# Hybrid decoder block: input rows transposed unscaled, row scales applied at evacuation, the next block's convolution placed ahead of the scan

## The chip, the cores and the metric

The kernel runs on one core of a Trainium2 chip. The metric is the device time of one execution in microseconds (us), median of the runs.

## The reference

All in float32, 1024 tokens of width 1024:

```
h = RMSNorm(x);  [u_rnn | g_rnn | u_pool | q_mem] = h @ W_in        (1024 x 1536)
A (512 ch): u = causal depthwise conv(4)(u_rnn) + b
            r, i = sigmoid(u @ W_a + b_a), sigmoid(u @ W_i + b_i)   (per head, 64x64)
            a = exp(-8 r softplus(-lam)); h_t = a h_(t-1) + sqrt(1 - a^2) i u;  y = h * gelu(g_rnn)
B (256 ch): trailing means over 2/4/8/16 tokens minus the token, a map per group, a scale
C (256 ch): 4 heads of q_mem attend to keys and values of RMSNorm(mem) (256 rows)
x = x + concat(A, B, C) @ W_out;   x = x + MoE(RMSNorm(x))  (top 4 of 32 experts);  out = RMSNorm(x)
```

## The kernel before, in words

The program has two phases: the mixer (everything up to the router and the token lists, about the first 350 us) and the expert phase, which starts when the mixer is done. The change touches the mixer alone. Each engine has its own program, written out by hand, and runs it in order; semaphores join them, so the order of the text is the order of the work.

**Three products for one.** The large products are made as hi*hi + hi*lo + lo*hi: a float32 operand is split in a rounded part (a copy on ScalarE, "hi") and a rest (a subtraction on VectorE, "lo"). One projection `n` of the input matrix has 128 output channels: two halves of 512 tokens, 8 k-steps of three products each, so 24 products a half (L1057 to L1059).

**The head.** Ten row tiles of 128 rows (8 of `x`, 2 of `mem`) are loaded by SP into 7 slots. ScalarE squares and sums each tile (`square`, L429), VectorE makes the mean (L711), ScalarE the root (L434), VectorE the reciprocal (L707), ScalarE scales the identity matrix by it (`row_scale`, L448), and TensorE multiplies the tile with that scaled identity (`transpose_rows`, L1039), which transposes and normalizes at once. ScalarE makes the hi part of a tile's first bank (`x_hi`, L439), VectorE the hi part of the second and both lo parts (`xT_evac`, L722, L725). A table of 50 columns of weights (`vrows`, eight small loads that POOL issues at L357) is transposed at L1072 before tile 2 and copied to `vec` (L702); POOL scales the first two pieces of W_in by a column of it (L381, `scale`), ScalarE and VectorE split them (`w_in_hi` L457, `w_in_lo` L734). The first half of projection 0 comes after the transposes of tile 7.

**Keys and values.** SP loads the key/value weights (2 MB, L288) into the place of tiles 3 to 6 once they are transposed, then eight pieces of a bias (L291, L292), then W_in piece by piece (L274), each when its slot of three is free. VectorE scales pieces 2 and up (L738). `keys_values` (L1082, L1086) follows projection 1, and ScalarE copies its result out (L599, L601).

**The recurrence.** Four blocks `c` of 128 channels. TensorE: projection 2c (u), projection 2c+1 (g), then `gates(c)` (L1099, from the convolved u), with no pause between them; they need w_in_lo of the piece, and the banks of two projections before emptied. ScalarE: `root_of(c-1)` (L515), `u_evac(c)` (L486), w_in_hi(2c+2), `g_evac(c)` with the gelu (L496), w_in_hi(2c+3), `gate_values(c)` (sigmoid L504 and L506, tanh L509, exp L510), each change of function with a table load. VectorE, for each c: w_in_lo(2c+3); i*u (L826); L829 to L832; scale(2c+5); L835, L836, the scan (L837), the product with the gelu (L841, semaphore `rnn_done`); `conv(c+1)` (L807, L810); w_in_lo(2c+4); scale(2c+6).

**After it.** Projections 8 and 9 (pool), 10 and 11 (queries) are interleaved with the pooling windows (`pool_windows`, VectorE), the first scores and the split of W_out. Then eight token tiles go through the output product, second norm and router, and TensorE is fed without a gap until the mixer's end.

Of the kernel before, what the change touches and what calls it, by code (L numbers as in the profile page):

```python
# [67 lines left out]
def mixer_phase(nc, dram, scratch, shared):  # L68

    ctx = ExitStack()  # L70
    with ctx:
# [32 lines left out]
        def c_tile(i):  # L104
# [42 lines left out]
        scales = nc.alloc_sbuf_tensor_at("scales", [P, 2, P], F32, offset=start["b_gu_lo"])  # L147
# [3 lines left out]
        w_out_row = [rows[:, 0, :], rows[:, 1, :], rows[:, 2, :], w_out_h[:, :],  # L151
# [21 lines left out]
        gexp = sb("gexp", [P, TOPK])  # L173
        cnt = sb("cnt", [P, 8, E])
# [4 lines left out]
        ss2, ms2, sd2, rs2 = (small[:, 40 + i * 2:42 + i * 2] for i in range(4))  # L179


        rows_in = [sem(f"rows_in{i}") for i in range(7)]
# [6 lines left out]
        vecT_ready, vec_done, lam_abs, lam_exp, lam_done = (sem(n) for n in ("vecT_ready", "vec_done", "lam_abs", "lam_exp", "lam_done"))  # L189
        ss_done, ms_done, sd_done, xn_done, xT_ready, xT_done = (sem(n) for n in ("ss_done", "ms_done", "sd_done", "xn_done", "xT_ready", "xT_done"))  # L190
# [6 lines left out]
        out_ready, x2_done, ss2_done, ms2_done, sd2_done, h2_done, h2T_ready, h2T_done = (  # L197
            sem(n) for n in ("out_ready", "x2_done", "ss2_done", "ms2_done", "sd2_done", "h2_done", "h2T_ready", "h2T_done"))
# [10 lines left out]
        rs_done = sem("rs_done")  # L209
# [4 lines left out]
        row_slots = [rows[:, i, :] for i in range(3)] + [region_d[:, i * D:(i + 1) * D] for i in range(4)]  # L214

        def row_slot(item):

            n = len(row_slots)
            if item < NORMED:
                return item % n, item // n + 1  # L220
            return (item - NORMED) % 3, sum(i % n == (item - NORMED) % 3 for i in range(NORMED)) + (item - NORMED) // 3 + 1

        def row_tile(item):
            return row_slots[row_slot(item)[0]]
# [37 lines left out]
        def _(sp):  # L262
            def load_rows(item):

                if item < TT or item >= NORMED:
                    t = item if item < TT else item - NORMED
                    src = dram["x"][0, t * P:(t + 1) * P, :]
                else:
                    src = dram["mem"][0, (item - TT) * P:(item - TT + 1) * P, :]
                sp.dma_start(row_tile(item), src).then_inc(rows_in[row_slot(item)[0]], 16)  # L270
# [23 lines left out]
            for n in range(3, NPROJ):  # L294
# [9 lines left out]
                if n == 8:  # L304
                    sp.wait_ge(bias_set, 16 * 8)
                    for k in range(RT):
# [7 lines left out]
            load_w_out(6)  # L314
            sp.wait_ge(d_done, 2)
            load_w_out(7)
            sp.wait_ge(w_out_lo_done, KT + 3)
# [21 lines left out]
        def _(pool):  # L339
# [6 lines left out]
            vector_rows = [  # L346
                (V_CONVW, CONV * RT, dram["conv_w"][0].rearrange("w (c p) -> (w c) p", p=P)),
                (V_CONVB, RT, dram["conv_b"][0].rearrange("(c p) -> c p", p=P)),
                (V_BA, RT, dram["b_rg_a"][0].rearrange("(c p) -> c p", p=P)),
                (V_BI, RT, dram["b_rg_i"][0].rearrange("(c p) -> c p", p=P)),  # L350
                (V_LAM, RT, dram["lru_lambda"][0].rearrange("(c p) -> c p", p=P)),
                (V_PS, PT_, dram["pool_scale"][0].rearrange("(c p) -> c p", p=P)),
                (V_GMIX, KT, dram["norm_mix_g"][0].rearrange("(c p) -> c p", p=P)),
                (V_GMEM, KT, dram["mem_norm_g"][0].rearrange("(c p) -> c p", p=P)),
            ]
            for r, n, src in vector_rows:
                pool.dma_start(vrows[r:r + n, :], src).then_inc(vrows_in, 16)  # L357
# [66 lines left out]
        def _(act):  # L424
            def square(s):
                act.wait_ge(rows_in[row_slot(s)[0]], 16 * row_slot(s)[1])
# [5 lines left out]
            def root(s):  # L432
                act.wait_ge(ms_done, s + 1)
                nc.scalar.activation(sd[:, s:s + 1], ms[:, s:s + 1], ACT.Sqrt).then_inc(sd_done, 1)  # L434

            def x_hi(s):

                act.wait_ge(xT_ready, s + 1)
                nc.scalar.activation(hi_part[:, 0:4, s * P:(s + 1) * P],  # L439
                                     bank(4 + 2 * (s % 2))[:, 0, :].rearrange("p (k t) -> p k t", k=4),  # L440
                                     ACT.Copy).then_inc(x_hi_done, 1)

            def row_scale(s):

                if s >= 2:
                    act.wait_ge(xT_ready, s - 1)
                act.wait_ge(rs_done, s + 1)
                nc.scalar.activation(scales[:, s % 2, :], ident[:, :], ACT.Copy, scale=rs[:, s:s + 1]).then_inc(xn_done, 1)  # L448
# [9 lines left out]

            act.preload_act_table(ACT.Sqrt)
            square(0)  # L460
            square(1)
            act.wait_ge(consts, 1)
            root(0)
            for s in range(NORMED):
                if s + 2 < NORMED:
                    square(s + 2)
# [1570 lines left out]
```

## Time and profile before

| what | value |
|---|---|
| median of 3 runs | 1742.6 us (1738.94 to 1742.95) |
| the profiled execution, its own time | 1743.29 us |
| its span in the profile | 1741.6 us |
| TensorE busy | 1667.9 us, 96% of the span |
| VectorE / ScalarE / POOL busy | 75% / 63% / 27% |
| mean granted TensorE clock | 0.98 |

The profile gives one execution, in us from the start of the span. A row of the timeline has start, duration, engine, line, operation, output and inputs, count, and in brackets the idle time before it and what ended it. A busy TensorE is not one at its peak, since the durations of pipelined products overlap: the pace is read from start to start.

### The profile page before, as it was taken

The page shows a single profiled execution, that of the slowest core. Times are in us where ns is not written, and L with a number is a line of the kernel's source. Part 1 is how long each engine was busy: PE and PEld are TensorE (multiplying, and loading weights), DVE is VectorE, ACT ScalarE, POOL GpSimd, SP SyncE. Part 2 cuts the span into 40 slices and gives each one's busy share as a digit, 9 for nine tenths or more (in the row PEclk, how much of TensorE's full clock was granted, in tenths as well). Part 3 has the DMA queues.
Part 4 walks back from the last instruction along what each step waited for, and adds up shares of the span by engine and source line. Part 5 has one row for each costly group of instructions (what it writes and reads, how often), then busy time and mean ns, then how long its engine had stood idle before and what let it go on. Part 6 is the DMA issues. An engine that isn't in the chain of part 4 may idle for free.

```text
span 1741.6 us, 29439 instructions
## 1 busy us (share of the span) xinstructions
PE 1667.9 (96%) x8641; PEld 1242.4 (71%) x8642; DVE 1303.3 (75%) x1168; ACT 1103.9 (63%) x1074; POOL 463.9 (27%) x348
## 2 busy tenths in 40 slices
PE   6999999759999999999999999999999999999996
PEld 6877777546786768888868887678666767765674
DVE  5578656666787868998869997669668669665787
ACT  5455555355676758877758876567556657654674
POOL 5000002432322525322225222215213026123240
PEclk9999999869999999999999999999999999999998
DMA  9121132467898989999989998689868788887685
GB/s 281 52 97 58 52 110 73 170 237 288 329 346 326 350 316 350 389 380 385 391 321 351 390 375 324 232 347 378 307 263 296 299 326 324 296 319 259 227 324 218
DMA packets 114171, 485.64 MB, mean 279 GB/s; under 512 B 16430, under 2 KB 29040, under 8 KB 81360
## 3 DMA queue, kind: packets, MB, share of 16 engines
q1 hardware_dynamic: 96128, 445.58, 66.0%
q0 software_dynamic: 18000, 39.49, 9.3%
q8 instruction: 27, 0.44, 0.1%
q14 instruction: 16, 0.13, 0.0%
HBM read 451.79 MB, written 33.23 MB: 278 GB/s over the span
## 4 chain that ended last, share of the span: by engine, by line
PE 71%; DVE 3%; issue 2%; DMA 2%; ACT 1%; POOLq 0%; ACTq 0%; DVEq 0%; POOL 0%; SPq 0%
PE ps L1837 20%; PE ps L1839 18%; PE ps L1838 18%; PE ps L1852 6%; PE ps L1890 3%; DVE w_lo L1681 2%; PE ps L1810 2%; PE ps L1860 1%; DMA raw_weights<-in_w_down 1%; ACT w_hi L1535 1%; PE ps L1915 1%; DVE raw_weights L1782 0%; PE ps L1819 0%; DMA stand_in<-token_lists 0%; DVE raw_weights L1799 0%
## 5 line engine op out<-in xcount | busy, mean ns | idle before, releaser
L1681 DVE TENSOR_TENSOR w_lo<-raw_weights,w_hi 128x2048 fp32r<-128x2048 f32 x256 | 576.5, 2284 | 137.8 <-ACT w_hi L1535 137.8
L1535 ACT ACTIVATE w_hi<-raw_weights 128x2048 fp32r<-128x2048 f32 x256 | 485.5, 1911 | 219.7 <-DMA raw_weights<-in_w_gu 114.9
L1837 PE MATMUL ps<-w_hi,xT 128*128 128x512 f32 x1024 | 415.4, 406 | 10.7 <-issue 5.1
L1838 PE MATMUL ps<-w_lo,xT 128*128 128x512 f32 x1024 | 402.9, 393 | 0.0
L1839 PE MATMUL ps<-w_hi,xT 128*128 128x512 f32 x1024 | 402.4, 393 | 0.0
L1681 DVE TENSOR_TENSOR w_lo<-raw_more,w_hi 128x2048 fp32r<-128x2048 f32 x128 | 290.1, 2284 | 28.8 <-ACT w_hi L1535 28.2
L1837 PEld LDWEIGHTS ps<-w_hi,xT 128*128 128x128 f32 x1024 | 194.1, 190 | 91.4 <-issue 46.6
L1535 ACT ACTIVATE w_hi<-raw_more 128x2048 fp32r<-128x2048 f32 x128 | 244.2, 1908 | 0.3 <-DMA raw_more<-in_w_down 0.3
L1461 POOL DMA_INDIRECT x_rows<-h_rows,next_list x33 | 79.0, 2395 | 598.0 <-issue 598.0
L1839 PEld LDWEIGHTS ps<-w_hi,xT 128*128 128x128 f32 x1024 | 193.8, 189 | 42.7
L1838 PEld LDWEIGHTS ps<-w_lo,xT 128*128 128x128 f32 x1024 | 194.3, 190 | 36.7
L1837 PE MATMUL ps<-w_hi,hT 128*128 128x512 f32 x512 | 211.1, 412 | 1.0 <-DVE hT L1722 1.0
L1839 PE MATMUL ps<-w_hi,hT 128*128 128x512 f32 x512 | 201.0, 393 | 0.0
L1838 PE MATMUL ps<-w_lo,hT 128*128 128x512 f32 x512 | 199.8, 390 | 0.0
L1506 POOL DMA_INDIRECT acc_rows<-y,this_list x31 | 169.5, 5469 | 57.8 <-ACT y L1604 51.4
L1593 ACT ACTIVATE glu<-ps 128x512 f32<-128x512 f32 x64 | 38.2, 597 | 145.0 <-PE ps L1839 143.2
L1839 PEld LDWEIGHTS ps<-w_hi,hT 128*128 128x128 f32 x512 | 96.1, 188 | 22.1
L1837 PEld LDWEIGHTS ps<-w_hi,hT 128*128 128x128 f32 x512 | 96.1, 188 | 19.3 <-issue 1.5
L1838 PEld LDWEIGHTS ps<-w_lo,hT 128*128 128x128 f32 x512 | 96.5, 188 | 17.2
L418 POOL DMA_INDIRECT token_lists<-entry,sloti x32 | 32.7, 1023 | 284.5 <-DVE sloti L944 276.9
L1722 DVE TENSOR_TENSOR hT<-ps,hT 128x512 fp32r<-128x512 f32 x64 | 44.2, 691 | 61.3 <-ACT hT L1597 61.2
L1852 PE MATMUL ps<-raw_weights,xT_tail 128*32 128x512 f32 x720 | 82.6, 596 | 0.0
(318 smaller groups left out, 2134.9 us busy)
## 6 DMA issues: line engine op xcount, KB each, us to landing
raw_weights<-in_w_gu SPq DMA_DIRECT2D x192, 1024.0 KB
raw_more<-in_w_gu SPq DMA_DIRECT2D x64, 1024.0 KB, 6.7
raw_weights<-in_w_down SPq DMA_DIRECT2D x64, 1024.0 KB
raw_more<-in_w_down SPq DMA_DIRECT2D x64, 1024.0 KB, 11.6
rows<-in_x SPq DMA_DIRECT2D x12, 512.0 KB
w_in_sb<-in_w_in SPq DMA_DIRECT2D x12, 512.0 KB, 4.6
acc_rows<-region_c SPq DMA_DIRECT2D x8, 512.0 KB
h_rows<-region_c SPq DMA_DIRECT2D x8, 512.0 KB
```

Of the source, the lines that this page charges most:

```text
L1461: pool.indirect_dma_start(out=x_rows[:, :], out_offset=None, in_=scratch["h2"], in_offset=bass.IndirectOffsetOnAxis(ap=next_list[:, 0:1], ...
L1506: pool.indirect_dma_start(out=scratch["acc"], out_offset=bass.IndirectOffsetOnAxis(ap=this_list[:, 0:1], axis=0), in_=y[:, :], in_offset=N ...
L1535: S.activation(w_hi[:, j % RING, :], raw(j % RING), ACT.Copy).then_inc(hi_done, 1)
L1593: S.activation(glu[:, :], ps[:, 2 * half, :], ACT.Gelu_apprx_sigmoid).then_inc(glu_done, 1)
L1681: V.tensor_tensor(w_lo[:, j % RING, :], raw(j % RING), w_hi[:, j % RING, :].bitcast(F32), ALU.subtract).then_inc(lo_done, 1)
L1722: V.tensor_tensor(part[:, :, 1, :], rows_transposed(2 * half), part[:, :, 0, :].bitcast(F32), ALU.subtract)\
L1810: last = T.transpose(ps[:, 1 + 2 * half, k * P:(k + 1) * P], x_rows[:, (4 * half + k) * P:(4 * half + k + 1) * P], ident[:, :])
L1837: T.matmul(out, hi, hi_w, start=first, stop=False)
L1838: T.matmul(out, hi, lo_w, start=False, stop=False)
L1839: return T.matmul(out, lo, hi_w, start=False, stop=end)
L1852: last = T.matmul(ps[q * TAIL:(q + 1) * TAIL, BANK_TAIL + g, :].rearrange("p (a n) -> p a n", a=2), xT_tail[:, k, g * TAIL:(g + 1) * TAIL] ...
L1890: last = T.matmul(ps[(2 * h + e) * TAIL:(2 * h + e + 1) * TAIL, BANK_TAIL + g, :], hT_tail[:, 2 * (p - KT) + e, g, :], piece[:, e, h * HAL ...
```

## The change

- The row tiles are transposed as they are, by a transpose against the identity, as soon as they have landed. All ten tiles and W_in pieces 0 to 2 have a slot of their own and are loaded at once.
- ScalarE makes the hi parts of both banks, VectorE only the lo parts. ScalarE squares all ten tiles after that, in one run; mean, root and reciprocal are made once for the ten. VectorE puts the scales on diagonals (128x1024 and 128x256), TensorE multiplies them with a matrix of ones (`row_scales`), so that every partition has the row of scales, and ScalarE copies it out (`rs_row`).
- u, g, the pool's inputs and the keys are multiplied by that row when they leave their banks, on VectorE (`scaled`); before, ScalarE copied them. The gelu is now made in place from SBUF (`gate_of`). Queries get their scale through the exponential's scale operand; values in their copy.
- The first half of projection 0 is cut in four pieces behind tiles 4 to 7; projection 1 comes between and behind the transposes of the memory tiles. SP loads the key/value weights when seven tiles are transposed and squared.
- `u_evac(c+1)` and `conv(c+1)` stand on VectorE between L832 and scale(2c+5), ahead of the scan; `g_evac(c+1)` is the last of iteration c.
- ScalarE issues the eight small loads of `vrows`, which POOL issued.
- One piece of W_out is loaded later, into another slot.

Cut to its core:

```diff
@@ SP
-            for item in range(len(row_slots)):
+            for item in range(TT // 2):
                 load_rows(item)
-            for n in range(3):
-                load_w_in(n)
-                sp.wait_ge(xT_ready, n + 1)
-                load_rows(len(row_slots) + n)
-            sp.wait_ge(xT_ready, len(row_slots))
+            load_w_in(0)
+            for item in range(TT // 2, TT):
+                load_rows(item)
+            load_w_in(1)
+            for item in range(TT, NORMED):
+                load_rows(item)
+            load_w_in(2)
+            sp.wait_ge(xT_ready, 7)
+            sp.wait_ge(ss_done, 7)
             sp.dma_start(w_kv_sb, ...)
@@ ScalarE
             act.preload_act_table(ACT.Sqrt)
-            ...
+            act.wait_ge(pool_step, 3)
+            for r, n, src in vector_rows:
+                act.dma_start(vrows[r:r + n, :], src).then_inc(vrows_in, 16)
+            for s in range(TT):
+                x_hi(s)
+                if s == 4:
+                    w_in_hi(0)
+            w_in_hi(1)
             for s in range(NORMED):
-                ...
+                square(s)
+            act.wait_ge(ms_done, 1)
+            nc.scalar.activation(sd[:, 0:NORMED], ms[:, 0:NORMED], ACT.Sqrt).then_inc(sd_done, 1)
+            act.wait_ge(vec_done, 2)
             nc.scalar.activation(lam[:, 1, :], lam[:, 0, :], ACT.Exp, scale=-1.0).then_inc(lam_exp, 1)
+            row_scales()
+            def gate_of(c):
+                for h in range(2):
+                    act.wait_ge(g_scaled, 2 * c + h + 1)
+                    half = g_t[:, h * HALF:(h + 1) * HALF]
+                    nc.scalar.activation(half, half, ACT.Gelu_apprx_tanh).then_inc(gelu_done, 1)
             for c in range(1, RT):
                 root_of(c - 1)
-                u_evac(c)
                 w_in_hi(2 * c + 2)
-                g_evac(c)
+                gate_of(c)
                 w_in_hi(2 * c + 3)
                 gate_values(c)
@@ VectorE
+            def scaled(out, n, h, signal):
+                dve.wait_ge(proj_ready, 2 * n + h + 1)
+                cols = slice(h * HALF, (h + 1) * HALF)
+                V.tensor_tensor(out[:, cols], bank(2 * (n % 2) + h)[:, 0, :], rs_row[:, cols], ALU.mult).then_inc(signal, 1)
+            for s in range(TT):
+                xT_evac(s)
+                if s == 2:
+                    vector_columns()
+                    dve.wait_ge(vec_done, 1)
+                if s == 4:
+                    w_in_lo(0)
+            w_in_lo(1)
             scale(2)
+            xT_evac(TT)
             ...
+            row_roots()
+            xT_evac(TT + 1)
+            scale(3)
             ...
+            dve.wait_ge(rs_row_done, 1)
+            dve.wait_ge(pads_zero, 2)
+            u_evac(0)
             conv(0)
+            g_evac(0)
             ...
             w_in_lo(2)
             scale(4)
+            keys_evac()
             for c in range(RT):
                 ...
                 link(V.tensor_scalar(a_t, m_t, 1.0, None, ALU.add))
+                if c + 1 < RT:
+                    u_evac(c + 1)
+                    conv(c + 1)
                 scale(2 * c + 5)
                 ...
                 V.tensor_tensor(mixedT[:, c, :], m_t, g_t, ALU.mult).then_inc(rnn_done, 1)
-                if c + 1 < RT:
-                    conv(c + 1)
                 w_in_lo(2 * c + 4)
                 if c + 1 < RT:
                     scale(2 * c + 6)
+                    g_evac(c + 1)
+            pooled_evac(0)
             pool_windows(0)
             w_in_lo(N_Q + 1)
+            pooled_evac(1)
             pool_windows(1)
@@ TensorE
                 for k in range(KT):
-                    last = T.matmul(..., row_tile(s)[:, k * P:(k + 1) * P], scales[:, s % 2, :], start=True, stop=True)
+                    last = T.transpose(..., row_tile(s)[:, k * P:(k + 1) * P], ident[:, :])
-            for s in range(NORMED):
+            for s in range(TT):
                 if s == 2:
                     pe.wait_ge(vrows_in, 16 * 8)
                     T.transpose(bank(0)[:, 0, 0:V_N], vrows[0:V_N, :], ident[0:V_N, 0:V_N]).then_inc(vecT_ready, 1)
                 transpose_rows(s)
-                if s >= TT - 1 and s < NORMED - 1:
-                    project_half(0, s - TT + 1)
+                if s >= TT // 2:
+                    k = 2 * (s - TT // 2)
+                    project_half(0, 0, range(k, k + 2))
+            project_half(0, 1)
+            transpose_rows(TT)
+            project_half(1, 0)
+            transpose_rows(TT + 1)
+            project_half(1, 1)
+            row_scales()
@@ keys_values: the wait for xT_done goes, one for rs_row_done stands ahead of the values
@@ gates(0), second half
-                        pe.wait_ge(kv_done, 2)
+                        pe.wait_ge(kv_done, 2 * MT)
```

## Rows read from the trace of the kernel before

**Rows 1.** The page, busy time of each engine.

```profile
PE 1667.9 (96%) x8641; PEld 1242.4 (71%) x8642; DVE 1303.3 (75%) x1168; ACT 1103.9 (63%) x1074; POOL 463.9 (27%) x348
```

**Rows 2.** Waits of TensorE, 30 to 330 us: who, total us, times, longest.

```profile
PE ps L1144 <- DVE region_d L889: 0.4, 1, 0.4
```

**Rows 3.** Timeline, TensorE in the head.

```profile
10.29 5.71 PE L1039 MATMUL ps<-scales,rows 128*128 128x128 f32 x32 [10.29 <-ACT scales L448]
...
29.66 2.02 PE L1039 MATMUL ps<-scales,rows 128*128 128x128 f32 x16 [0.64 <-DVE lo_part L725]
...
38.71 0.48 PE L1057 MATMUL ps<-hi_part,w_in_split 128*128 128x512 f32 x1
```

**Rows 4.** DMA view, 0 to 70 us: issues, KB each, us from issue to landing.

```profile
region_d<-in_w_mem_kv SPq DMA_DIRECT2D x1, 2048.0 KB, 10.9
...
vrows<-in_mem_norm_g POOLq DMA_DIRECT2D x1, 4.0 KB, 6.4
```

**Rows 5.** Timeline, the other engines in the head.

```profile
5.86 0.50 POOL L357 DMA_DIRECT2D vrows<-in_mem_norm_g  x1
...
19.17 3.75 POOL L381 TENSOR_TENSOR w_in_sb<-w_in_sb,vec 128x1024 f32<-128x1024 f32 x2 [6.84 <-DVE vec L702]
...
19.74 0.69 DVE L725 TENSOR_TENSOR lo_part<-ps,hi_part 128x512 fp32r<-128x512 f32 x1 [0.66 <-ACT hi_part L439]
```

**Rows 6.** Timeline, TensorE, a transpose of one tile against the identity, and what follows.

```profile
226.05 1.09 PE L1180 MATMUL ps<-ident,region_c 128*128 128x128 f32 x8
226.90 0.48 PE L1187 MATMUL ps<-hi_part,mixed_hi 128*128 128x512 f32 x1
```

**Rows 7.** Timeline, TensorE: gates(0), and the first products of blocks 1 and 3.

```profile
70.74 3.60 PE L1099 MATMUL ps<-region_c,blockdiag 128*128 128x512 f32 x8
73.77 0.80 PE L1057 MATMUL ps<-hi_part,w_in_split 128*128 128x512 f32 x1
...
124.28 0.80 PE L1057 MATMUL ps<-hi_part,w_in_split 128*128 128x512 f32 x1
```

**Rows 8.** Windows of 2 us: busy time (x instructions), clock, DMA share, GB/s.

```profile
44.00:46.00 2.00, 2.00 (x19) 1.94 (x17) 0.00 (x0) 0.00 (x0) 0.00 (x0) 1.00 0.08 24
```

**Rows 9.** Timeline, SP: the issue of the key/value weights.

```profile
29.05 0.38 SPq L288 DMA_DIRECT2D region_d<-in_w_mem_kv  x1
```

**Rows 10.** Timeline, VectorE from scale(3) to conv(0).

```profile
47.44 1.22 DVE L738 TENSOR_TENSOR w_in_sb<-w_in_sb,vec 128x1024 f32<-128x1024 f32 x1
...
53.82 0.81 DVE L807 TENSOR_SCALAR region_c<-region_c,vec 128x1024 f32<-128x1024 f32 x1 [0.32 <-ACT region_c L486]
```

**Rows 11.** Timeline, VectorE in block 1 of the recurrence.

```profile
105.36 1.22 DVE L829 SCALAR_TENSOR_TENSOR region_c<-region_c 128x1024 f32<-128x1024 f32 x1 [2.36 <-ACT region_c L510]
...
109.21 1.23 DVE L738 TENSOR_TENSOR w_in_sb<-w_in_sb,vec 128x1024 f32<-128x1024 f32 x1
...
115.23 0.81 DVE L807 TENSOR_SCALAR region_c<-region_c,vec 128x1024 f32<-128x1024 f32 x1
...
119.91 1.22 DVE L734 TENSOR_TENSOR w_in_split<-w_in_sb,w_in_split 128x1024 fp32r<-128x1024 f32 x1
121.05 1.22 DVE L738 TENSOR_TENSOR w_in_sb<-w_in_sb,vec 128x1024 f32<-128x1024 f32 x1
```

**Rows 12.** Timeline, ScalarE in block 1 of the recurrence.

```profile
90.82 1.28 ACT L496 ACT_TABLE_LOAD   x1 [3.96 <-PE ps L1059]
92.11 0.60 ACT L496 ACTIVATE region_c<-ps 128x512 f32<-128x512 f32 x1
96.19 0.60 ACT L496 ACTIVATE region_c<-ps 128x512 f32<-128x512 f32 x1 [3.48 <-PE ps L1059]
...
97.75 1.28 ACT L504 ACT_TABLE_LOAD   x1
...
99.63 1.12 ACT L504 ACTIVATE region_c<-ps,vec 128x1024 f32<-128x1024 f32 x1 [0.59 <-PE ps L1099]
...
105.27 1.28 ACT L515 ACT_TABLE_LOAD   x1
```

More of the change, by code:

```diff
@@ L173, in mixer_phase @@
         gexp = sb("gexp", [P, TOPK])
+        mem_scale = [b[:, :, :].rearrange("p j e -> p (j e)") for b in (onehot, picked)]
+        rs_row = rows[:, 2, :]
+        rs_diag, mem_diag = m_t.rearrange("p (s t) -> p s t", s=TT), uc[:, 0:MT * P].rearrange("p (s t) -> p s t", s=MT)
         cnt = sb("cnt", [P, 8, E])
@@ L305, in _ @@
                     sp.wait_ge(bias_set, 16 * 8)
-                    for k in range(RT):
+                    for k in range(RT - 1):
                         load_w_out(k)
@@ L430, in square, with row_scales @@
                     .then_inc(ss_done, 1)
-            def root(s):
-                act.wait_ge(ms_done, s + 1)
-                nc.scalar.activation(sd[:, s:s + 1], ms[:, s:s + 1], ACT.Sqrt).then_inc(sd_done, 1)
             def x_hi(s):
                 act.wait_ge(xT_ready, s + 1)
[L439 to L448, printed above, removed]
+                for b in range(2):
+                    nc.scalar.activation(hi_part[:, 4 * b:4 * b + 4, s * P:(s + 1) * P],
+                                         bank(4 + 2 * (s % 2) + b)[:, 0, :].rearrange("p (k t) -> p k t", k=4),
+                                         ACT.Copy).then_inc(x_hi_done, 1)
+            def row_scales():
+                act.wait_ge(rs_row_ready, 1)
+                nc.scalar.activation(rs_row, bank(6, 2).rearrange("p b n -> p (b n)"), ACT.Copy).then_inc(rs_row_done, 1)
+                for m in range(MT):
+                    nc.scalar.activation(mem_scale[m], bank(5)[:, 0, m * P:(m + 1) * P], ACT.Copy).then_inc(rs_row_done, 1)
             def w_in_hi(n):
@@ L595, in _ @@
             nc.scalar.activation(shared["pick"][:, :, :], pick_in[:, :, :], ACT.Copy).then_inc(pick_done, 1)
-            g_evac(0)
+            gate_of(0)
             w_in_hi(3)
             act.wait_ge(kv_ready, 1)
-            nc.scalar.activation(kT[:, :, :], bank(4)[:, 0, :].rearrange("p (c m) -> p c m", c=2), ACT.Copy)\
-                .then_inc(kv_done, 1)
-            nc.scalar.activation(v_sb[:, :, :], bank(5)[:, 0, :].rearrange("p (c m) -> p c m", c=MT), ACT.Copy)\
-                .then_inc(kv_done, 1)
+            for m in range(MT):
+                nc.scalar.activation(v_sb[:, m, :], bank(5)[:, 0, m * D_XATTN:(m + 1) * D_XATTN], ACT.Copy,
+                                     scale=rs[:, TT + m:TT + m + 1]).then_inc(kv_done, 1)
+            act.wait_ge(pads_zero, 2)
+            act.wait_ge(zero_out, 32)
+            act.wait_ge(table_set, 16)
+            act.wait_ge(vec_done, 1)
+            act.wait_ge(lam_done, 2)
             gate_values(0)
@@ L1038, in transpose_rows, with row_scales @@
                 for k in range(KT):
-                    last = T.matmul(bank(4 + 2 * (s % 2) + k // 4)[:, 0, (k % 4) * P:(k % 4 + 1) * P],
-                                    row_tile(s)[:, k * P:(k + 1) * P], scales[:, s % 2, :], start=True, stop=True)
+                    last = T.transpose(bank(4 + 2 * (s % 2) + k // 4)[:, 0, (k % 4) * P:(k % 4 + 1) * P],
+                                       row_tile(s)[:, k * P:(k + 1) * P], ident[:, :])
                 last.then_inc(xT_ready, 1)
+            def row_scales():
+                pe.wait_ge(diag_done, 2)
+                pe.wait_ge(xT_done, 2 * NORMED)
+                pe.wait_ge(consts, 8)
+                for h in range(2):
+                    T.matmul(bank(6 + h)[:, 0, :], ones[:, :], m_t[:, h * HALF:(h + 1) * HALF], start=True, stop=True)
+                T.matmul(bank(5)[:, 0, 0:MT * P], ones[:, :], uc[:, 0:MT * P], start=True, stop=True).then_inc(rs_row_ready, 1)
             def project_half(n, h, ks=range(KT)):
```

199 lines of the change are left out of this document (82 added, 117 removed).

## The prediction

> **What bounds the kernel now.** I read the page first: TensorE is busy 96% of the span, no other engine above 75% [rows 1]. An average hides stages, so I looked at the waits of TensorE in the mixer. From 30 to 330 us the longest is 0.4 us [rows 2]: the mixer is fed without a pause once the first product starts. So a change to the mixer can gain in two ways only: start TensorE's products earlier, or give it less to do. Whatever it adds to the other engines is free until it uses up their slack. The timeline of the head then shows that TensorE does its first tile at 10.29 us, its first projection product at 31.44 and the second half of projection 0 at 38.71 [rows 3]. The expert phase follows the mixer's end, so I carry a shift of that end over to the whole, one for one.
>
> **The head, up to 38.71 us before.**
>
> 1. The scale chain ahead of each transpose goes. A tile costs 8 instructions and 0.85 us (226.05 to 226.90 [rows 6]) in place of 16 and 2.02 [rows 3].
> 2. The next lateness is the weight columns. ScalarE issues eight loads at 0.50 each, if they cost what POOL's do [rows 5], from about 2.3 to 6.3. No load issued by ScalarE is in the trace: the nearest row took 6.4 us to land [rows 4] under the same flood of row tiles, another queue could be 3 us faster, and I take 5.5 from the last issue, so 11.3. TensorE stands before tile 2 until then. Bounds: 8.6 and 13.5.
> 3. Their transpose and tile 2, at the slow early pace (32 in 5.71, or 0.178 each, against 0.127 [rows 3]), hi and lo parts of two halves (0.6 and 0.69 each, [rows 5, 12]): 15.0. Copy to `vec` 15.2, POOL's scale 1.87 (two in 3.75 [rows 5]) 17.1, w_in_hi 1.05 (96.19 plus 0.6 to 97.75 [rows 12] less overlap) 18.2, w_in_lo 1.22 [rows 11] 19.5.
> 4. From tile 4 on TensorE waits in its own order for that w_in_lo. Behind it stand 24 products at 0.23 (96 in a period of 25.25 less 3.03 for the gates [rows 7]; 5.5) and three tiles (2.6), and because it idled I add 1.8 for products at half pace; below that nothing, above it 3. Tile 7's last parts end at 30.2. The second half of projection 0 thus starts at 30.2 instead of 38.71: **8.5 gained**.
> 5. From there to the first product of block 1 it was 35.06 (38.71 to 73.77 [rows 3, 7]). The last memory tile is 0.85 cheaper, another one now stands behind 38.71's place (0.85 more), and four scale instructions of 512 at 0.38 (eight gate products in 3.03 [rows 7]) and two of 256 at 0.43 add 2.4: **2.5 lost**.
> 6. ScalarE squares after the last hi parts: ten at about 1.25 end near 43, roots and diagonals near 45, TensorE asks for them at 48.6. Hidden, with 3.4 to spare. But SP sends the 2 MB of key/value weights only after seven squares, at 39.2, needed at 51.0; 10.9 to land [rows 4], so just in time. The bias pieces and W_in piece 3 follow. Before, that whole batch ran from 29.05 [rows 9] until the DMA engines fell quiet at 44 [rows 8], with POOL's and the last row's transfers in it; alone I give it 11.5, so piece 3 lands at 50.7 (bounds 48 and 53).
> 7. VectorE now has scale(3) in front of everything. From it to conv(0) took 6.4 [rows 10], less 0.3 of wait, then u 1.3, conv 4.68 [rows 11], g 1.3, bias 1.2, w_in_lo(2) and scale(4) 2.3, keys 0.8: 68.4. The second half of gates(0) wants the keys at 66.3. **2.1 lost** (bounds 0 and 4).
>
> Block 1 starts 8.5 - 2.5 - 2.1 = 3.9 us earlier.
>
> **The recurrence.** TensorE's period was 25.25 (two in 73.77 to 124.28 [rows 7]), and conv(c+1) was done 1.3 before gates(c+1) asked: moving it ahead of the scan buys nothing by itself. What counts is a loop that the change closes. ScalarE's gelu of c+1 now waits for VectorE's `g_evac(c+1)`, the last thing in iteration c, and `gate_values(c+1)` stands behind that gelu. From one sigmoid to the next:
>
> - sigmoid to L829: 99.63 to 105.36, 5.73 [rows 11, 12]
> - L829 to L832: 105.36 to 109.21, 3.85 [rows 11]
> - u's two halves, 0.6 and 0.69 like L725 [rows 5]: 1.3; conv: 115.23 to 119.91, 4.68 [rows 11]
> - scale, scan, product: 109.21 to 115.23, 6.02 [rows 11]
> - w_in_lo and scale: 1.14 each [rows 11], 2.3; g's halves 1.3
> - second gelu half and w_in_hi, 96.19 to 97.75: 1.56; sigmoid's table load 1.28 [rows 12]
>
> Sum 28.1, against TensorE's 25.25. The first round also waits 0.7 for the second half of u. Count each block from TensorE's first product: sigmoid 0 starts 0.6 in, sigmoid 1 4.2 in, and w_in_lo(2c+4) ends 22.8 after a sigmoid. Block 1: 27.0 where 25.25 is wanted, **1.8 lost**; sigmoid 2 then starts 5.2 in, block 2: 28.1, **2.9 lost**; block 3 does without u and conv, but the pool's input is multiplied on VectorE behind w_in_lo(10), so projection 10 starts at 22.8 where 22.2 is wanted, and the windows and second pool input follow as closely: 0.6 + 0.6 = **1.2 lost**. Together 5.9. The late piece of W_out lands well ahead of its use.
>
> A rule weighed here: what a change of tables costs. The row shows 1.28 and the gelu starting 1.29 after the load's start (90.82 to 92.11 [rows 12]). The Trainium skill (ScalarE: Activation LUTs, What ACT_TABLE_LOAD costs) adds a drain of about 1.38 us to each switch. By the rows the sum keeps 1.28; by that figure the three sigmoid loads on the loop would add an estimated 4.1. The trace speaks against it.
>
> **Sum.** -3.9 + 5.9 = +2.0 on the profiled execution's 1743.3, so 1745.3; that execution stands 0.7 above the median of 1742.6, and I say 1745.0.
>
> **The rivals.**
>
> *A, the fast head.* The columns land at 8.6, by the time of the third tile (2.2 us sooner at step 4), TensorE is at full pace (1.8) and piece 3 comes early enough for the keys (2.1). For: ScalarE's loads need not queue as POOL's did. Against: the same row tiles flood the DMA engines. Gives 1745.3 - 6.1 = 1739.2. With a loop shorter than summed it passes the bound for faster. Chance 0.24.
>
> *B, the gelu's table load behind its wait, slower.* Before, that load started at 90.82, when the bank was ready, not earlier [rows 12]. If it does so again behind `g_scaled`, in every block from 1 to 3, it lengthens the closed loop by 1.28 three times, 3.8: 1749. It decides as soon as the load starts later than VectorE's first half of g. Against: the square root's load, with one wait ahead like the new gelu, went out at once (105.27 [rows 12]). Chance 0.12.
>
> *C, late key/value weights or piece 3.* Each us beyond 50.7 is a us on gates(0); 3 more give 1748. Chance 0.10.
>
> *D, the table change costs a drain.* As a mechanism of this kernel: the sigmoid starts over a us after its load ends, each block, and the mixer ends 4 later: 1749. The rows show no such gap. That rule is the one named above. Chance 0.04.
>
> *E, the loop isn't there,* because TensorE's slack takes it: then -3.9 alone, 1739.4. Both programs are in order and TensorE had no wait to give [rows 2], so little. Chance 0.05.
>
> The forecast as worked out keeps 0.45.
>
> **How the numbers follow.** A measurement can tell about 0.3% from no change, 5.2 us: faster means below 1737.4, slower above 1747.8. The forecast alone covers 1741 to 1749 from its bounds (step 2 by 2, step 6 and 7 by 2, each loop term by 0.3), and with a fifth of its chance it is slower. Faster takes half of A and some of E and of errors in the head: 0.16. Slower takes most of B, D, half of C and that fifth: 0.26. Same 0.58. The range from 1737 to 1750 reaches into A and E below and takes in B and D above.
>
> **What would show it.** Right: the second half of projection 0 near 30; TensorE idle some 3 to 4 us ahead of tile 5, waiting for w_in_lo; gates(0) waiting a little for the keys; in blocks 1 and 2 waits of TensorE for w_in_lo of 2 to 3 us, with sigmoids about 28 apart. Wrong: sigmoids 25 apart and no such waits (then faster, as E); waits of over 4 (then B or D); keys' products waiting for their DMA (C). A different expert phase would make the whole reading wrong.

## The result, and the profile after

The changed kernel is slower, by more than was forecast: 1749.9 us (median of 7 runs, 1747.3 to 1754.1) against 1742.6 of before on the same chip (7 runs, 1736.1 to 1743.9), a ratio of 1.0055 with a 95% interval of 1.004 to 1.007. The ratio is taken over all runs, by their means 1750.5 and 1740.9, so it says 9.6 us where the two medians say 7.3. The forecast was 1745.0. One run of a kernel below ("squares early", 1907 us at a mean granted clock of 0.84) is a slow one, and its ratio leaves it out. The profiled execution took 1753.1 with a span of 1751.2, against 1743.3 and 1741.6 before.

From the page of the changed kernel, as in [rows 1]: busy time of the engines, the DMA queues that carry programs, and the first group of expert products.

```profile
PE 1667.3 (95%) x8567; PEld 1238.2 (71%) x8568; DVE 1312.5 (75%) x1167; ACT 1101.8 (63%) x1054; POOL 454.2 (26%) x340
...
q8 instruction: 41, 0.67, 0.2%
...
L1871 PE MATMUL ps<-w_hi,xT 128*128 128x512 f32 x1024 | 416.7, 407 | 16.3 <-issue 13.2
```

The same two lines on the page of before:

```profile
q8 instruction: 27, 0.44, 0.1%
...
L1837 PE MATMUL ps<-w_hi,xT 128*128 128x512 f32 x1024 | 415.4, 406 | 10.7 <-issue 5.1
```

TensorE is as busy as it was and has 74 matmuls less, but it stands idle longer: before the expert products there are 13.2 us in which it waited for nothing that the profile shows, against 5.1. And queue 8, which carries instructions, moved 41 packets of 16 KB instead of 27.

**The mixer.** The timeline of TensorE in the head, which answers to [rows 3]:

```profile
4.51 3.43 PE L1057 MATMUL ps<-ident,rows 128*128 128x128 f32 x16 [4.51 <-DMA rows<-in_x]
10.52 0.26 PE L1099 MATMUL ps<-ident,vrows 50*128 50x50 f32 x1 [2.57 <-DMA vrows<-in_mem_norm_g]
...
19.42 0.79 PE L1084 MATMUL ps<-hi_part,w_in_split 128*128 128x512 f32 x1 [3.38 <-DVE w_in_split L749]
...
30.96 0.47 PE L1084 MATMUL ps<-hi_part,w_in_split 128*128 128x512 f32 x1 [0.67 <-issue]
```

The first product comes at 19.42 and the second half of projection 0 at 30.96. Further on, the gates of block 0 and the first products of blocks 1 to 3, as in [rows 7] (TensorE), and ScalarE's part of the loop, as in [rows 12]:

```profile
69.67 1.98 PE L1133 MATMUL ps<-region_c,blockdiag 128*128 128x512 f32 x4 [2.64 <-DVE kT L743]
...
71.08 0.79 PE L1084 MATMUL ps<-hi_part,w_in_split 128*128 128x512 f32 x1
...
96.32 0.80 PE L1084 MATMUL ps<-hi_part,w_in_split 128*128 128x512 f32 x1
...
124.01 0.50 PE L1084 MATMUL ps<-hi_part,w_in_split 128*128 128x512 f32 x1 [1.87 <-DVE w_in_split L749]
...
152.09 0.50 PE L1084 MATMUL ps<-hi_part,w_in_split 128*128 128x512 f32 x1 [2.59 <-DVE w_in_split L749]
```

```profile
73.05 1.11 ACT L497 ACTIVATE region_c<-ps,vec 128x1024 f32<-128x1024 f32 x1
...
84.06 1.28 ACT L490 ACT_TABLE_LOAD   x1
97.64 1.23 ACT L490 ACTIVATE region_c<-region_c 128x512 f32<-128x512 f32 x2 [12.30 <-DVE region_c L715]
98.78 1.04 ACT L457 ACTIVATE w_in_split<-w_in_sb 128x1024 fp32r<-128x1024 f32 x1
99.84 1.28 ACT L497 ACT_TABLE_LOAD   x1
101.14 1.12 ACT L497 ACTIVATE region_c<-ps,vec 128x1024 f32<-128x1024 f32 x1
```

Block 1 starts 2.7 earlier than before (71.08 for 73.77). The gelu of block 1 waited 12.30 us for VectorE's `g_evac`, and from sigmoid to sigmoid it takes 28.09, so TensorE waits for `w_in_lo` at 124 and 152. The mixer's end, taken as the start of the last eight transposes of h2, moves from 332.12 to 335.95: +3.8.

```profile
335.95 1.97 PE L1214 MATMUL ps<-ident,region_c 128*128 128x128 f32 x8 [2.70 <-DVE region_c L931]
```

**The expert phase.** The rest, 5.8 of the profiled 9.6, arose in code that the change does not touch: from the mixer's end to the end of the span it was 1409.5 before and is 1415.3. Counted from the first expert product the difference is larger. Before it was

```profile
372.17 0.79 PE L1837 MATMUL ps<-w_hi,xT 128*128 128x512 f32 x1 [1.49 <-DVE xT L1687]
```

and in the changed kernel it is

```profile
373.75 0.79 PE L1871 MATMUL ps<-w_hi,xT 128*128 128x512 f32 x1 [1.49 <-DVE xT L1721]
```

so the loop starts only 1.6 later, and from there to the end it takes 1377.4 where it took 1369.4. That is 8.0 more, while the idle time without a releaser grew by 8.1. (The stretch between the two marks, with the routing tables and the first gather, was 2.2 shorter here. It takes 37.7 to 40.3 in the profiles below, and what sets it was not looked into.) The clearest place is behind the last unit with two tails (a unit is one round of the expert loop, in a variant with no, one or two tails, short extra groups of tokens). TensorE in the timeline, and in windows (columns as in [rows 8]); then what the DMA view of 1574 to 1640 us has for queue 8:

```profile
1629.83 0.39 PE L1873 MATMUL ps<-w_hi,hT 128*128 128x512 f32 x1
1636.35 0.79 PE L1871 MATMUL ps<-w_hi,xT 128*128 128x512 f32 x1 [6.13 <-issue]
1636.93 0.63 PE L1872 MATMUL ps<-w_lo,xT 128*128 128x512 f32 x1
```

```profile
1628.00:1632.00 4.00, 2.22 (x10) 1.49 (x8) 3.94 (x4) 3.95 (x4) 2.47 (x2) 1.00 0.13 18
1632.00:1642.00 10.00, 5.65 (x13) 4.13 (x13) 7.53 (x5) 4.55 (x4) 5.33 (x2) 0.52 0.58 110
```

```profile
q8 instruction: 7, 0.11, 0.7%
```

TensorE ends a unit at 1629.83 and begins the next one only at 1636.35, with nothing named as the reason. The DMA records have instruction packets that start at 1627.9, 1631.0, 1633.5 and 1636.5. The third has landed at 1634.4, TensorE goes on 2.0 later, and the fourth starts 0.2 behind that: the packets lie in and around the pause, but none ends at the very moment when it does. Behind it the granted clock is 0.52, so nearly all at its lower level of 1.2 GHz, and a product takes 630 ns instead of 390. Before, the same hand-over from one unit to the next took 0.9, the clock stayed at 1.00, and there was no packet between 1121 and 1714. (The kernel before has a shorter pause of this kind too: 3.13 us without a releaser ahead of 1121.21, behind three packets.)

### The profile page after: what moved, and what is told of

Its sections match the earlier page's. It is cut to its first block, busy times and chain, and to the rows that moved or that the text cites. A ratio compares the mean times of both kernels' runs of the same rounds, so it can differ in the third digit from the quotient of the medians.

```text
span 1751.2 us, 29257 instructions
## 1 busy us (share of the span) xinstructions
PE 1667.3 (95%) x8567; PEld 1238.2 (71%) x8568; DVE 1312.5 (75%) x1167; ACT 1101.8 (63%) x1054; POOL 454.2 (26%) x340
## 4 chain that ended last, share of the span: by engine, by line
PE 69%; DVE 4%; DMA 3%; issue 2%; ACT 1%; POOLq 0%; ACTq 0%; DVEq 0%; POOL 0%; SPq 0%
PE ps L1871 19%; PE ps L1873 18%; PE ps L1872 18%; PE ps L1886 6%; PE ps L1924 3%; DVE w_lo L1715 3%; DMA raw_weights<-in_w_down 2%; PE ps L1844 2%; PE ps L1894 1%; ACT w_hi L1569 1%; PE ps L1949 1%; DVE raw_weights L1816 0%; PE ps L1853 0%; DMA stand_in<-token_lists 0%; DVE y_tail L1793 0%
## 5 line engine op out<-in xcount | busy, mean ns | idle before, releaser
L1871 PE MATMUL ps<-w_hi,xT 128*128 128x512 f32 x1024 | 416.7, 407 | 16.3 <-issue 13.2
L1569 ACT ACTIVATE w_hi<-raw_more 128x2048 fp32r<-128x2048 f32 x128 | 244.0, 1907 | 0.1
```

The lines of the kernel that those rows point to most:

```text
L1569: S.activation(w_hi[:, j % RING, :], raw(j % RING), ACT.Copy).then_inc(hi_done, 1)
L1871: T.matmul(out, hi, hi_w, start=first, stop=False)
```

## The experiments

The kernels ran in three jobs, each on a chip of its own. In each job the kernel before ran on the same chip; the ratios are to it. Its medians were 1743.6 in the first job, 1740.4 in the second and 1740.6 in the third. The first job asks how much of the time is the mixer's, the others why the expert phase got longer.

**The loop in the recurrence, undone.**

```diff
-            gate_of(0)
             w_in_hi(3)
...
                 root_of(c - 1)
+                gate_of(c - 1)
                 w_in_hi(2 * c + 2)
-                gate_of(c)
                 w_in_hi(2 * c + 3)
                 gate_values(c)
             root_of(RT - 1)
+            gate_of(RT - 1)
```

> Change kept, but ScalarE makes block c's gelu behind its square root instead of ahead of the sigmoids of the same block. Theory L (the loop from sigmoid through VectorE's g to the gelu and back, 28.09 us long in the changed kernel, costs TensorE its waits of 1.9 and 3.4 us for w_in_lo): sigmoids 25.2 to 25.5 apart, these waits gone or under 0.5 us, TensorE's first tile of the expert phase about 5 us earlier than in the changed kernel, total ratio to the kernel before near 1.002. Rival V (VectorE is simply full: 23 us of work and 2.4 of waiting in 25.25): sigmoids stay over 27 apart and the waits stay within 1 us of what they were, whatever the place of the gelu.

Measured: 1749.2, ratio 1.0041 (1.0024 to 1.0058). The sigmoids are 25.25 apart and the waits for `w_in_lo` in the recurrence are gone. (Of the two waits that the expectation names, 3.4 is that of the head, ahead of 19.42; those of the loop are 1.87 and 2.59.) The mixer ends at 332.13, 3.8 earlier than with the change, although W_in piece 3 landed 2.2 later in this execution (55.0 for 52.8) and block 1 started at 73.32 instead of 71.08. From block 1 on the gain is thus 6.0: the loop is real and costs what was worked out, 5.9. But the whole gained only 0.14%, less than its interval can tell: in the profiled execution (1756.0; the runs go from 1742.7 to 1758.3) TensorE stood still for 8.4 us at one place of the expert phase. Its timeline there:

```profile
1344.76 0.79 PE L1871 MATMUL ps<-w_hi,xT 128*128 128x512 f32 x1 [8.43 <-issue]
```

**The squares early.** Four squares behind `w_in_hi(0)`, then one behind each tile's hi parts, so that SP sends the key/value weights sooner.

```diff
                     w_in_hi(0)
+                    for r in range(4):
+                        square(r)
+                elif s > 4:
+                    square(s - 1)
             w_in_hi(1)
-            for s in range(NORMED):
+            for s in range(TT - 1, NORMED):
                 square(s)
```

> Change kept, but ScalarE squares tiles 0 to 6 in the gaps between the hi parts (four behind w_in_hi(0), then one behind each tile) instead of all ten at the end. Theory K (the key/value weights wait for seven squares, and W_in piece 3 behind them holds VectorE up to 52.8 us, so that the keys come 2.6 us late for the gates of block 0): key/value weights issued near 31 instead of 39.6, scale(3) near 45 to 47 instead of 52.8, the wait of 2.6 us for the keys gone, first product of block 1 near 68.4 instead of 71.1. As the loop of the recurrence is untouched, 2 to 2.7 us remain of it at the mixer's end. Rival: another piece (the bias copies, the values' copy, hi parts held up by the squares) is as late, and under 1 us is gained.

Measured: 1749.7, ratio 1.0040 (1.0022 to 1.0059). The key/value weights go out at 31.26, TensorE no longer waits for the keys, block 1 starts at 68.31 (68.4 said), sigmoid 0 starts 2.8 earlier and the mixer ends at 333.69, 2.3 earlier. The time hardly follows here either.

**Both.** The two edits above together.

> Both edits of the two runs before in one. If the two costs are separate, the gains add: mixer's end 7 to 8 us earlier than in the changed kernel, 3 to 4 earlier than in the kernel before, ratio 0.995 to 0.999 if the expert phase goes as in the kernel before. If the expert phase of the changed kernel is longer by some 6 us for a reason that has nothing to do with these two (its code, its positions), the ratio is near 1.001 in spite of the earlier mixer's end.

Measured: 1743.8, ratio 1.0011 (0.9998 to 1.0024). The mixer ends at 325.68, 6.4 earlier than before and 10.3 earlier than with the change alone, and still the kernel is no faster than before. The expert phase takes 1414.5, again 5.0 more than before's.

**Before, started later.** Four memsets on POOL ahead of everything, and SP waits for them.

```diff
+            for i in range(4):
+                pool.memset(r_pad, 0.0).then_inc(pad_done, 1)
+                pool.wait_ge(pad_done, i + 1)
...
+            sp.wait_ge(pad_done, 4)
```

> The kernel before, with all loads and POOL's work held back by four memsets of about 1 us, so that the whole mixer runs 4 us later and nothing else is changed. Theory S (a shift of the mixer's end goes one for one to the whole, and the expert phase of the changed kernel is longer because of its own code): +4 us, ratio 1.0023. Theory P (the length of the expert phase depends on where in time it falls, by TensorE's clock drops at the pauses between experts): a total that is more than 2 us away from +4, like the +9 of the changed kernel.

Measured: 1746.5, ratio 1.0020 (1.0004 to 1.0035). The mixer ends 3.2 later and the span is 3.1 longer: an expert phase of 1409.3, as before's 1409.5, with 27 packets. So a later start does not by itself lengthen the expert phase. Something else of the changed kernel does.

The theory that came out of the trace (F): the change takes 74 matmuls and their 74 weight loads out of TensorE's program (16 instead of 8 a tile for ten tiles, less six for the row of scales). The program of the expert loop then lies otherwise in the pieces in which it is fetched. In the mixer of before, four packets lie at 132.8, 163.5, 191.4, 218.0 and the next at 235.7; the windows between them hold 513 matmuls and 509 weight loads, 256 for each packet:

```profile
132.80:163.50 30.70, 30.70 (x130) 24.05 (x129) 24.32 (x24) 18.68 (x20) 0.00 (x0) 1.00 0.06 18
163.50:191.40 27.90, 27.90 (x122) 21.71 (x121) 22.43 (x29) 11.13 (x23) 0.00 (x0) 1.00 0.28 95
191.40:218.00 26.60, 26.16 (x149) 19.37 (x147) 16.86 (x27) 16.10 (x41) 0.00 (x0) 1.00 0.17 60
218.00:235.70 17.70, 17.69 (x112) 13.76 (x112) 7.29 (x11) 10.28 (x21) 0.00 (x0) 1.00 0.25 90
```

The Trainium skill (Runtime: NRT & Kernel Launch, Instruction fetch mechanics) says that an engine's program is fetched in blocks of 16 KB, 256 instructions, that TensorE's memory for it holds 2048, and that a taken branch to a target outside the current window of two blocks stalls the engine until that block is fetched. The packets agree with the block size. A window of only two blocks does not fit the trace of before: from 1121 to 1714 TensorE ran 3190 matmuls and 3190 weight loads in 13 rounds of the loop, through all three variants of its branch, without one packet; a round with two tails alone ran 715 of them. No run here shows how many blocks TensorE holds.

**More instructions for TensorE.** The next runs put one-by-one matmuls of `ones` at the end of TensorE's mixer program, where it waits for the routing tables. Each is two matmuls and two weight loads. Their result goes to a place of PSUM that nobody reads.

```diff
             rank(TT - 1)
+            for _ in range(37):
+                T.matmul(bank(0)[0:1, 0, 0:1], ones[:, 0:1], ones[:, 0:1], start=True, stop=True)
             pe.wait_ge(slot_done, TT)
```

The changed kernel with 37 of them:

> The changed kernel with 37 one-by-one matmuls of ones at the end of TensorE's mixer program, where it waits for the routing tables; each is two matmuls and two weight loads, so its program up to the expert loop is 148 instructions longer and about as long as before's. The mixer is not touched (its last h2 tile stays at about 336, 3.8 later than before). Theory F (the expert phase got longer because TensorE's shorter program lies otherwise in what is fetched of it): the 14 added instruction packets (41 against 27) go away, unit 33 takes 46 again instead of 54, the clock stays up, the total falls by 3 to 6 to about 1745 to 1747 (ratio to before 1.001 to 1.002, what the mixer's shift alone gave in the run of before 4 us later). Rival R (semaphores, ScalarE's DMA queue or another engine's program): nothing but the 37 matmuls changes, total 1749 to 1751, ratio 1.004 or more, unit 33 still 54, 41 packets.

Measured: 1759.1, ratio 1.0120 (1.0097 to 1.0144), worse by far than without them. The mixer's end stays (335.17); the expert phase takes 1421.2. Neither F as I had sized it nor its rival R expected this.

The kernel with both moves and the same 37:

> The kernel with both moves of ScalarE's program (gates behind roots, squares early; mixer's end 6.4 earlier than before) and the same 37 matmuls. Theory F: expert phase as before's, 27 packets, so that the total is 5 to 7 below before: about 1737, ratio 0.996. Rival R: as without them, 1743.8, ratio 1.001.

Measured: 1749.9, ratio 1.0068 (1.0042 to 1.0094), expert phase 1421.5: worse as well. Both are 37 matmuls in a stretch in which TensorE waits: they delay nothing there (with both moves x_rows of unit 1 is gathered at 355.20 with and without them, with the change alone at 362.74 with and 363.69 without). And yet they cost about 10 us later on (1.0120 for 1.0055, 1.0068 for 1.0011). Something about their number is wrong, and it matters.

The kernel before with 27, 108 instructions:

> The kernel before with 27 such matmuls, 108 instructions: as an instruction packet carries 16 KB, and TensorE's packets come about every 256 instructions, this puts before's expert loop where the changed kernel's lies within a packet (148 less is 108 more, up to one packet). The mixer is before's (332). Theory F with position within a packet deciding: expert phase 5 to 7 longer, about 40 packets, total 1748 to 1750, ratio 1.003 to 1.004. If only the length (how many packets stand ahead of it) decides, or Rival R: 27 packets, ratio 1.000.

Measured: 1745.7, ratio 1.0032 (1.0016 to 1.0048), 45 packets, an expert phase of 1414.4. The kernel before, with nothing of the change in it, gets the changed kernel's pause at the same place:

```profile
q8 instruction: 45, 0.74, 0.2%
...
L1839 PE MATMUL ps<-w_hi,xT 128*128 128x512 f32 x1024 | 415.5, 406 | 17.9 <-issue 16.4
```

```profile
1631.16 0.79 PE L1839 MATMUL ps<-w_hi,xT 128*128 128x512 f32 x1 [6.83 <-issue]
```

By the exact count given further down, its loop begins three instructions ahead of the changed kernel's place and not on it. Here that makes no difference that can be told. The run ends rival R: neither semaphores, nor ScalarE's DMA queue, nor another engine's program is needed for it.

The changed kernel with 64, one whole packet:

> The changed kernel with 64 such matmuls, 256 instructions, one whole packet. Theory F with the position within a packet: nothing changes against the changed kernel, 41 packets and one for the added code, ratio 1.004. With any longer program helping: as with 37 of them, ratio 1.001 to 1.002. Rival R: ratio 1.004 as well, so this run decides only together with that of 37.

Measured: 1750.5, ratio 1.0069 (1.0045 to 1.0093), 42 packets at the changed kernel's places, an expert phase of 1412.4. A longer program helps nothing as such; a shift by a whole packet changes nothing that can be told.

**The exact position.** The count of 148 left out that the changed kernel's TensorE program has some wait instructions more. The traces have 98 waits of TensorE up to the first expert product before and 101 after the change, so its program is 145 instructions shorter and not 148. Counted with those, 37 matmuls put the expert loop three instructions behind before's. So 36 of them, and three satisfied waits, which come to one instruction (the page counts 29257 instructions without this filling and 29402 with it, 145 more):

```diff
+            for _ in range(36):
+                T.matmul(bank(0)[0:1, 0, 0:1], ones[:, 0:1], ones[:, 0:1], start=True, stop=True)
+            for _ in range(3):
+                pe.wait_ge(consts, 9)
             pe.wait_ge(slot_done, TT)
```

> The kernel with both moves on ScalarE, with 36 one-by-one matmuls and 3 satisfied waits at the end of TensorE's mixer program: 36 times 4 and 3 wait instructions fall short of 148 by as much as the changed kernel has more waits, so that its expert loop begins at the very instruction number of before's (37 matmuls overshot it by 3). Theory F (exact position decides): 27 instruction packets as in before, mixer's end at about 326, expert phase 1409.5 as in before, total 1735 to 1737, ratio 0.996. If the position is not what sets it (chance of each run, or another engine's program): 1743 to 1750 as without or with 37, ratio 1.001 or more.

Measured: **1735.4, ratio 0.9971 (0.9957 to 0.9985)**, faster than both kernels. Its page:

```profile
q8 instruction: 27, 0.44, 0.1%
...
L1879 PE MATMUL ps<-w_hi,xT 128*128 128x512 f32 x1024 | 414.7, 405 | 10.9 <-issue 5.4
```

The packets are 27, the idle time 5.4, the expert phase 1404.3. Two kernels further down, with both moves as well and other positions, ran in the same job and came to 1741.8 and 1742.9. The stretch in which the changed kernel lost 6 us lies 10 earlier here; a window of it shows full clock and 0.93 of idle time:

```profile
1618.00:1628.00 10.00, 9.07 (x64) 4.19 (x64) 9.50 (x8) 6.52 (x6) 5.99 (x4) 1.00 0.46 147
```

The changed kernel with the same filling:

> The changed kernel with the same 36 matmuls and 3 waits. Theory F: 27 packets, mixer's end at 336, expert phase 1409.5: total 1746 to 1747, ratio 1.002 (the mixer's 3.8 alone). Otherwise 1749.5 or more, ratio 1.004 and up.

Measured: 1745.7, ratio 1.0026 (1.0010 to 1.0043), 27 packets, idle time 5.2, expert phase 1407.3. This is the change alone, with the position of the loop held: by the ratio 4.5 us more than before (1.7 to 7.5). The profiled execution took 1748.0 and is one of the slower half of twelve (1741.2 to 1744.0 and 1747.4 to 1752.5). Its first expert product:

```profile
376.63 0.79 PE L1875 MATMUL ps<-w_hi,xT 128*128 128x512 f32 x1 [1.50 <-DVE xT L1725]
```

That is 4.5 later than before, and from there to the end it takes 1369.3, as before's 1369.4: all of its difference stands ahead of the loop. Its mixer ends 2.7 later than in the changed kernel's profile, though the code is the same: W_in piece 3 landed at 54.2 instead of 52.8, and TensorE was granted 0.56 of its clock from 72 to 74 and 0.54 from 154 to 156, behind waits of 3.28 and 2.58, where the changed kernel's profile has 1.00 behind 2.64 and 2.59. So the mixer's 3.8 is the figure of one execution.

Two more positions for the kernel with both moves, 16 and 54 matmuls:

> The kernel with both moves and 16 such matmuls: its expert loop begins 64 instructions later, 79 past a multiple of 256 where the changed kernel's is at 15 and before's at 160. A look at how the price goes with the position; Theory F only says that it may be anything from before's (total 1736) to the worst seen (1750), and that packets and total go together: under 30 packets with 1738 or less, over 38 with 1742 or more. Without F: 1743.8.

Measured: 1741.8, ratio 0.9998 (0.9979 to 1.0017), 35 packets. That lies between the two cases, for which fewer than 30 and more than 38 had been named, and the time does too, nearly: above 0.9971 at before's place and, by less than the intervals can tell, below 1.0011 without filling. Its twelve runs go from 1731.4 to 1744.3, and the packets are known of one of them (1742.1) alone.

> The same with 54 matmuls, 216 instructions, 231 past a multiple of 256. As above: packets and total go together; without F 1743.8.

Measured: 1742.9, ratio 1.0016 (1.0003 to 1.0030), 42 packets.

The profiles side by side, in us; "from there on" is the span less the column before it, and the last column is the "issue" idle time ahead of the first group of expert products:

| kernel | mixer's end | from there on | first expert product | from there on | q8 packets | issue |
|---|---|---|---|---|---|---|
| before | 332.1 | 1409.5 | 372.2 | 1369.4 | 27 | 5.1 |
| before, 4 us later | 335.4 | 1409.3 | 375.3 | 1369.5 | 27 | 5.7 |
| change, exact position | 338.7 | 1407.3 | 376.6 | 1369.3 | 27 | 5.2 |
| both moves, exact position | 327.0 | 1404.3 | 364.7 | 1366.6 | 27 | 5.4 |
| both moves, 64 on | 326.3 | 1413.8 | 364.4 | 1375.7 | 35 | 10.9 |
| change + 64 matmuls | 336.6 | 1412.4 | 374.8 | 1374.3 | 42 | 14.5 |
| before + 27 matmuls | 331.2 | 1414.4 | 369.6 | 1375.8 | 45 | 16.4 |
| squares early | 333.7 | 1414.4 | 374.0 | 1374.2 | 44 | 14.6 |
| both moves | 325.7 | 1414.5 | 365.4 | 1374.8 | 41 | 13.7 |
| change | 336.0 | 1415.3 | 373.8 | 1377.4 | 41 | 13.2 |
| both moves, 216 on | 326.2 | 1415.4 | 363.9 | 1377.7 | 42 | 17.8 |
| change + 37 matmuls | 335.2 | 1421.2 | 372.9 | 1383.5 | 43 | 12.7 |
| both moves + 37 | 327.5 | 1421.5 | 365.5 | 1383.5 | 41 | 8.9 |
| gelu behind root | 332.1 | 1422.0 | 372.2 | 1381.9 | 43 | 20.8 |

All kernels with 27 packets need 1404 to 1410 us for the expert phase, all others 1412 to 1422; from the first expert product on it is 1366.6 to 1369.5 against 1374.2 to 1383.5. In the two rows with 37 matmuls part of the pause is booked on VectorE's `w_lo` (7.4 and 9.3) and not on "issue".

## Why the prediction was wrong

**The step that failed** is the first one: "The expert phase follows the mixer's end, so I carry a shift of that end over to the whole, one for one." It had weighed only the time at which that phase starts, and put a change of the phase itself at nothing. For a shift in time it holds: the kernel before started 4 us later had its mixer's end 3.2 later and grew by 3.1. But the change also shortens TensorE's program ahead of the expert loop, and at the new place the loop costs about 5 us more. Two comparisons of ratios give it: the change as it is against the change at before's position, 1.0055 against 1.0026, 0.29% or 5.1 us; the kernel before against itself 108 instructions on, 1.0032, 5.6 us. With both moves it is 0.40% (1.0011 against 0.9971), 7.0 us. In the profiles, from the first expert product on, these three are 8.1, 6.4 and 8.3. Step 1 of the head counted those instructions, 8 for 16 a tile, and asked only what time they save. "A different expert phase would make the whole reading wrong" named the sign but no rival had it, and no chance stood behind it. That the median 1749.9 still lies inside the range from 1737 to 1750 is luck: its upper end was drawn for rivals B and D, and neither happened.

**The mixer** went the way it was worked out, +3.8 at its end for +2.0 (and +1.6 at the first expert product, by a shorter routing stretch):

- Head. First product 19.42 (19.5 said), second half of projection 0 at 30.96 (30.2), the vector columns' transpose at 10.52 (by 11.3). The columns were 0.8 early and the way from them to the first product 0.7 longer than summed, so two errors cancel in the 19.42. TensorE was granted 0.53 from 20 to 25 us, and had a pause of 0.67 with no releaser. From the first product to the second half it took 0.8 more than the sum, which had 1.8 for slow products and nothing for a pause:

```profile
20.00:25.00 5.00, 5.00 (x18) 4.18 (x17) 0.28 (x1) 0.91 (x2) 4.08 (x7) 0.53 0.67 215
```

- Keys. SP issued the key/value weights at 39.55 (39.2). W_in piece 3 landed at 52.8 (50.7, near the bound of 53), but VectorE caught up most of it: gates(0) waited 2.64 instead of 2.1. So block 1 starts 2.7 earlier, not 3.9.
- The loop. Its length was summed to 28.1 and is 28.09. Block 1 lost nothing (71.08 to 96.32 is 25.24); the waits come one block later, 1.87 and 2.59, and 0.8 twice at queries and attention, 6.1 in all (6.5 by the mixer's end), where 5.9 was said in the order 1.8, 2.9, 1.2.
- The rivals. Not A: the columns came at 10.52 and not at 8.6, and the piece for the keys was late, not early. Not B: the gelu's table load went out at 84.06 and had ended 12.30 before the gelu's wait did. Not D: the sigmoid starts 1.30 after its load does, in all four blocks (1.29 in the last). C in its small form, 0.5. E not at all.

So the terms of the mixer were off by 1.8 together, 1.2 in the head with the keys and 0.6 in the loop. With the loop at before's position the change costs 1.0026, 4.5 us, where the forecast had 2.4 (1745.0 for 1742.6), which is inside that ratio's interval of 1.7 to 7.5. Of the 9.6 us that the ratio 1.0055 says, the other 5.1 are the loop's place.

**What stays open.** Shown is that the number of TensorE's instructions ahead of the loop moves the time of the loop, and that more packets and longer pauses without a releaser go with it. That TensorE waits in these pauses for its program is argued from the packets in and around them; the profile names no releaser. Open is which rule makes one position cheap and another dear. The price isn't steady in it: from before's place three instructions on it is among the worst seen (1421), while three ahead of the changed kernel's place it is much the same as on it; 64 past the changed kernel's it is 35 packets, and a whole packet on it is the same as without. Nor is it the number of packets alone, for the kernels with 41 to 45 lie between 1412 and 1422. Most of that spread is a pause of 6.2 to 8.4 us near 1340, which showed in three of the profiled executions. It came with "gelu behind root" but not with the change itself or "squares early", which have the same TensorE program, so it is also a matter of timing between executions; how often it comes was not measured. Nor is it known why both moves at the exact position need 1366.6 from the first expert product on, 2.8 less than before with the same 27 packets. A shorter loop was not tried.

## What to carry to other kernels

In this kernel, which ends in a long loop with branches, an edit ahead of the loop that changes the number of TensorE's instructions moved the time by 0.3 to 0.9% without touching the loop. Look at the packets of the instruction queue on both pages before explaining a difference, and judge an edit with the count of instructions held equal. A mixer 6 us shorter counted for nothing until the loop was back at a good place; both together gave 0.9971. And a single profile gives a stretch of the mixer only to some 3 us: the same mixer ended at 335.2 to 338.7 in four kernels.

## What the runs showed that I had not expected

- From before's place, three instructions more ahead of the loop cost 13 to 15 us by the medians (of different jobs, in which before had 1740.6 and 1740.4): 1735.4 against 1749.9 for both moves, 1745.7 against 1759.1 for the change.
- The pause of 6 us costs more than its length: behind it the granted clock was at its lower level (0.52 from 1632 to 1642, and 0.93 from 1642 to 1646).
- Eight loads issued by ScalarE landed sooner than I had said, since they went out sooner: from 1.48 to 4.24, at 0.26 to 0.57 each and not 0.50. From the last issue to TensorE's transpose it took 6.3, and not 5.5. And the transposes against the identity ran so fast that TensorE idled and was granted 0.53 of its clock when the first products came. So part of what the head saved came back as slower products.
